# A two-block transformer kernel: rows kept in natural column order through the expert layers

## What is computed

```python
h = jnp.concatenate([meta, x], axis=1)                     # 16 + 256 rows of 1024
for i in range(2):
    h = layer_norm(ALPHA * h + mixed, ln_g[i, 0], ln_b[i, 0])
    # experts: router on h, two experts per token, blocks of gathered rows
    #   hb = silu(xb @ w_gate[e]) * (xb @ w_up[e]);  y += gate * (hb @ w_down[e])
    ffn = hierarchical_moe(h, w_group, b_group, w_expert, b_expert, w_gate, w_up, w_down)
    h = layer_norm(ALPHA * h + ffn, ln_g[i, 1], ln_b[i, 1])
x = h[:, 16:]                                              # then the second block
```

## Time and profile before

| | |
|---|---|
| median of 3 runs | 2130.85 us |
| the three runs | 2118.84, 2130.85, 4760.82 us |
| the profiled execution | 2120.57 us, its span 2118.8 us |
| TensorE busy (matmuls) | 1641.4 us, 77% of the span |
| VectorE busy | 624.1 us, 29% |
| ScalarE busy | 219.3 us, 10% |
| moved by DMA | 546.00 MB, mean 258 GB/s |
| mean granted TensorE clock | 0.869 of full speed |

### The profile page before, as it was taken

One profiled execution on the slowest core, in us unless ns is written; L12 is line 12 of the kernel. 1 busy time (PEld: TensorE's weight loads), 2 busy tenths in 40 slices (PEclk: granted clock), 3 DMA queues, 4 the chain that ended last, 5 costly groups with the idle time before them and its releaser, 6 DMA issues.

```text
span 2118.8 us, 27169 instructions
## 1 busy us (share of the span) xinstructions
PE 1641.4 (77%) x12015; PEld 1066.4 (50%) x12015; DVE 624.1 (29%) x1449; ACT 219.3 (10%) x488; POOL 171.5 (8%) x173
## 2 busy tenths in 40 slices
PE   7897767776766997466556553668999998999998
PEld 5544444444445855243334322336688445668743
DVE  4633122322213763111111115992211012421002
ACT  2301010000001321000000001000011002311000
POOL 2000100000000000000000002991000001000000
PEclk9985988989898997787778776658999999899999
DMA  9352999999999574999999996122434424323420
GB/s 315 119 199 82 336 419 422 419 422 419 421 421 351 210 294 167 419 418 417 419 418 417 419 423 270 40 80 99 173 126 159 144 92 143 118 102 142 154 79 20
DMA packets 105219, 546.00 MB, mean 258 GB/s; under 512 B 7406, under 2 KB 9518, under 8 KB 86924
## 3 DMA queue, kind: packets, MB, share of 16 engines
q1 hardware_dynamic: 102572, 534.39, 63.6%
q0 software_dynamic: 2528, 9.84, 1.3%
HBM read 534.77 MB, written 9.44 MB: 257 GB/s over the span
## 4 chain that ended last, share of the span: by engine, by line
PE 57%; DMA 29%; DVE 8%; issue 3%; SPq 1%; ACT 1%; POOL 0%; DVEq 0%; POOLq 0%; ACTq 0%
DMA ring<-in_moe_w_up 29%; PE ps L664 16%; PE ps L640 16%; PE ps L685 9%; PE ps L1001 3%; PE ps L705 2%; PE ps L697 2%; PE ps L648 2%; DVE work L1911 2%; PE ps L714 1%; DVE work L1910 1%; DVE work L1900 1%; PE ps L1040 1%; DVE work L1901 1%; SPq L423 1%
## 5 line engine op out<-in xcount | busy, mean ns | idle before, releaser
L685 PE MATMUL ps<-ring,work 128*32 128x256 f32 x3968 | 297.2, 466 | 285.1 <-DMA ring<-in_moe_w_up 284.0
L685 PEld LDWEIGHTS ps<-ring,work 128*32 128x32 f32 x3968 | 166.2, 133 | 412.0 <-issue 371.3
L664 PE MATMUL ps<-ring,work 128*128 128x512 f32 (+1 forms) x800 | 346.7, 596 | 13.1 <-DVE work L1830 9.2
L640 PE MATMUL ps<-hT,ring 128*128 128x256 f32 (+2 forms) x1488 | 330.9, 385 | 3.4 <-DMA ring<-in_lru_w_in 3.4
L640 PEld LDWEIGHTS ps<-hT,ring 128*128 128x128 f32 x1488 | 284.4, 192 | 48.5 <-issue 6.7
L664 PEld LDWEIGHTS ps<-ring,work 128*128 128x128 f32 (+1 forms) x800 | 149.0, 187 | 208.0 <-issue 202.4
L1701 DVE TENSOR_TENSOR rowb<-rowb,ps 128x128 f32<-128x128 f32 x64 | 18.4, 288 | 448.3 <-ACT rowb L1226 448.3
L697 PE MATMUL ps<-ring,multi 128*32 128x256 f32 x2016 | 121.8, 382 | 13.5 <-ACT multi L1228 12.8
L705 PE MATMUL ps<-rowb,hres 128*128 128x128 f32 (+1 forms) x640 | 107.9, 311 | 8.0 <-DVE rowb L1453 8.0
L1703 DVE COPY multi<-ps 128x256 f32<-128x256 f32 x64 | 27.2, 424 | 280.3 <-PE ps L697 280.3
L705 PEld LDWEIGHTS ps<-rowb,hres 128*128 128x128 f32 (+1 forms) x640 | 89.2, 204 | 25.1 <-DVE rowb L1453 8.3
(11 more groups left out here) (382 smaller groups left out, 1488.2 us busy)
## 6 DMA issues: line engine op xcount, KB each, us to landing
ring<-in_moe_w_down SPq DMA_DIRECT2D x63, 2048.0 KB, 24.2
ring<-in_moe_w_gate SPq DMA_DIRECT2D x62, 2048.0 KB, 19.4
ring<-in_moe_w_up SPq DMA_DIRECT2D x62, 2048.0 KB, 24.0
ring<-in_w_ff SPq DMA_DIRECT2D x32, 2048.0 KB, 8.4
ring<-in_sc_w_in SPq DMA_DIRECT2D x6, 2048.0 KB, 17.8
ring<-in_lru_w_in SPq DMA_DIRECT2D x4, 2048.0 KB, 18.7
s_rotations<-work POOLq DMA_DIRECT2D x8, 1024.0 KB, 5.1
ring<-s_rotations SPq DMA_DIRECT2D x4, 2048.0 KB, 15.4
```

The costliest lines, as they stand in the source:

```text
L640: mm = pe.matmul(ps[:, bank, 0:n], w[:, k, P * c:P * c + P], hT[:, k, t0:t0 + n], start=(k == 0), stop=(k == DC - 1))
L664: mm = pe.matmul(ps[0:m, 2 + 2 * b + hf, :], left[:, kk, t0:t0 + m], w[:, k, 512 * hf:512 * hf + 512], start=(kk == 0), stop=(kk == 4 * la ...
L685: mm = pe.matmul(ps[32 * q:32 * q + 32, bank, 0:256].rearrange("p (u n) -> p u n", u=2), x[:, k, :], gu[:, k, :, P * q:P * q + P], start=( ...
```

## The change

The rows of an expert layer stay in natural column order. The mix norms write `hres` plainly. The stationary matrices of the mix norms' transposes and of `dispatch` are taken at a stride instead: slab k is `hres[0:m, b, k:D:DC]`, every eighth column. `hT` and the gathered rows hold the same values as before. The residual sum reads `hres` in order, in one instruction per block, with the four PSUM banks as a second dimension. The copy of the meta rows and its wait are gone; TensorE turns them out of `hres` directly.

```diff
-        meta_rows = region(1024, 1024)[0:NMETA]
...
-        def packed(ap):
-            return ap.rearrange("t (p k) -> t k p", k=DC)
-        def unpacked(ap):
-            return ap.rearrange("t (k p) -> t p k", k=DC)
         def two(ap, k):
-            return ap.rearrange("t (a b) -> t a b", b=k)
+            return ap.rearrange("t (a b) -> t a b", a=k)
...
-            def transposes(n, blocks, hold, only=None, bank=0):
+            def transposes(n, blocks, hold, only=None, bank=0, by=1):
...
-                        for c in range(4):
-                            mm = pe.transpose(ps[:, bank + j % 2, c * P:c * P + m], hres[0:m, b, (4 * h + c) * P:(4 * h + c + 1) * P],
+                        for c in range(4 * h, 4 * h + 4):
+                            chunk = slice(c * P, c * P + P) if by == 1 else slice(c, D, by)
+                            mm = pe.transpose(ps[:, bank + j % 2, (c % 4) * P:(c % 4) * P + m], hres[0:m, b, chunk],
                                               ident[0:m, 0:m])
...
-                        mm = pe.matmul(ps[:, bank, width * (k - k0):width * (k - k0) + width], hres[0:m, b, P * k:P * k + P],
+                        mm = pe.matmul(ps[:, bank, width * (k - k0):width * (k - k0) + width], hres[0:m, b, k:D:DC],
                                        one_hot[0:m, i, 0:width], start=(i == 0), stop=(i == len(blocks) - 1), skip_group_check=True)
...
-                    transposes(f"mix{l}", blocks, f"mix{l}_normed", only=i)
+                    transposes(f"mix{l}", blocks, f"mix{l}_normed", only=i, by=DC)
...
-                        pe.wait_ge(*nth("meta_rows", 1))
                         for c in range(DC):
-                            mm = pe.transpose(ps[:, 6, NMETA * c:NMETA * c + NMETA], meta_rows[:, P * c:P * c + P], ident[0:NMETA, 0:NMETA])
+                            mm = pe.transpose(ps[:, 6, NMETA * c:NMETA * c + NMETA], hres[0:NMETA, 0, P * c:P * c + P], ident[0:NMETA, 0:NMETA])
...
-            def to_packed(x, dst, bias):
-                return packed(x), two(dst, P), packed(bias)
...
-                mix_norm(f"mix{l}", to_packed)
+                mix_norm(f"mix{l}")
...
-                    if l == 0 and e == 0:
-                        V.tensor_copy(two(meta_rows, DC), unpacked(hres[0:NMETA, 0, :])).then_inc(S("meta_rows"), 1)
...
-                    for q in range(4):
-                        ins = V.scalar_tensor_tensor(out=x[:, 256 * q:256 * q + 256].rearrange("t (p k) -> t p k", k=DC),
-                                                     in0=unpacked(hres[:, b, :])[:, 32 * q:32 * q + 32, :], scalar=ALPHA,
-                                                     in1=ps[:, q, SEQ * i:SEQ * i + SEQ].rearrange("t (p k) -> t p k", k=DC),
-                                                     op0=ALU.mult, op1=ALU.add)
-                    link(ins)
+                    link(V.scalar_tensor_tensor(out=two(x, 4), in0=two(hres[:, b, :], 4), scalar=ALPHA,
+                                                in1=ps[:, 0:4, SEQ * i:SEQ * i + SEQ], op0=ALU.mult, op1=ALU.add))
```

## The result

| kernel | median us | range | ratio to before, 95% interval |
|---|---|---|---|
| before | 2124.74 (9 runs) | 2118.84 to 2130.85, one of 4760.82 | 1 |
| changed | 2134.61 (9 runs) | 2129.39 to 2139.36 | 1.0047 [1.0029, 1.0064] |

The forecast was a gain of 3 us; the change costs 10. The time lies inside the forecast range and within 2% of before, but the direction was wrong. The execution of 4760.82 us is left out of the ratio. The spans of the two profiled executions are 2129.6 and 2118.8 us. They differ by 10.8, about as the medians do, so the traces can be laid side by side.

The account below looks back on a forecast made before the run. The weight stream bounds the expert loops; single-file work before and after it bounds the rest. VectorE gains of 3.26 us less 0.2 us for strided loads gave -3.1 us from 2120.57, so 2117.5 us, range 2112 to 2139.

Parts of the forecast that it names:

- VectorE's gains: Plain mix norm writes save 1.58 us and one-piece residual sums in layer 1 save 1.68 us, together 3.26 us.
- Layer 0's residual: Residual sum after layer 0's experts: about 0.84 us saved per block, hidden behind TensorE's work, so gain nothing.
- The price of one load: Strided stationary loads on TensorE: 0.91 ns per value, free cold, 5 ns extra for each of 32 warm loads, 0.2 us.
- the bound from two streams: All 1.81 ns per value charged to a strided TensorE load: 232 ns a load, 5.4 us in all.
- rival 1: Small price: TensorE's strided loads pay what VectorE pays for strides, +5.5 us against -3.26, 2122.8 us; chance 27%.
- The slack of the loops: Expert loops: TensorE slack of 107 and 152 us absorbs added dispatch time; only one in-loop dispatch, in layer 1, counts.
- 420 GB/s as before: Weight stream inside the expert loops keeps its rate of 420 GB/s.
- the three signs of being wrong: Cold strided load clearly over 213 ns; stream drying up at other places; layer 0's L910 coming earlier.
- First dispatch of layer 0: Forecast 15.0 us; about 16 to 17.5 under rival 1, about 25 under rival 2.
- Warm loads: Strided loads in layer 1's dispatch at the high clock: period of 111 to 116 ns, against 160 to 232.
- rival 2: Double loads: each of the 112 counted dispatch and transpose loads twice as long, +20.6 us, kernel 2137.9 us; chance 12%.
- The clock: Granted clock steps may be caught earlier or later by shifted stages: a few us either way, 1.6 us in layer 1's dispatch.

Follow-up runs that it names:

- the loads alone: Whole computation left out, TensorE alone running fp32 products and transposes at several column distances; a product's load at distance 8 took 238 ns for 128 columns.
- the best version: Changed kernel with ScalarE copying the two large blocks so their dispatch loads are contiguous, and in-loop dispatch behind down: 2119.04 us, 0.9969 of before.

## Why the prediction was wrong, step by step

- **VectorE's gains: right.** 1285 ns for 2077, and one residual for four. Layer 0's residual was hidden as said: there L901 (L910 before) starts at 666.88 against 666.32. Up to 816 us the change is 0.25 us ahead. The two norm writes gave their 1.58 us and layer 0's first dispatch took 1.2; the rest is a start 0.7 us ahead by scatter (146.65 against 147.36), 0.4 us in layer 0's first gate and up, and 0.5 us lost by the end of its loop.
- **The price of one load: wrong by a factor of two.** This is the first step that failed. The text took 0.91 ns per value, since "a load is one stream", and had 1.81 ns as the bound from two streams. Measured are 1.86. The error was to read the copy L1705, one stream on VectorE, as the nearest row. TensorE's own instructions spoke already: in the kernel before, at the higher clock, a product's load takes 111 ns and a transpose of the meta rows 62, so a product's load is not like one stream. By the forecast's own count the term is then 80 x 27 + 32 x 127 ns = 6.2 us instead of 0.2 (16 of the 80 are transposes, which cost nothing; without them 5.8), and the sum 2123.5 us: rival 1, given 27%.
- **The Trainium skill's rule was the right warning.** First the rows: distance 2 takes 118 ns, 3 173, 4 233, 16 218. With fp32, two neighbouring values at a distance of 2 share 16 bytes, and from a distance of 4 none do. At a distance of 3 one pair in four values shares them, and 173 ns is halfway between 112 and 233. The Trainium skill's Advanced Engine Details and Errata, section SBUF Cachelines, states such a rule: lines of 16 bytes, two hits needed on each to hide the memory's latency, and a penalty where every access falls on another line. The trace agrees for products on where the step lies; the page gives no price. For transposes the trace has no such step (120 ns at distances 2 and 4, 110 at 8), so it is not shown that the rule is the mechanism. The forecast cited it and gave it weight only in the rivals.
- **The slack of the loops: the second step that failed**, and the larger one. The forecast put the dispatches inside the loops at nothing: it divided a whole loop's slack (107 us in layer 0) by its loads and counted a single dispatch of layer 1. The runs put 9 to 10 us on them. But slack is not the same everywhere: the issue of the next down load waits for down, down stands behind the dispatch in TensorE's queue, and in layer 1 the gate and up loads queue behind that down load on SP. So 2.0 us are added to one chain in each group of four experts, and the stream was barely kept full there (375 GB/s at 911 to 914 us in the kernel before). The forecast saw this place once, at 848 us, and did not ask whether it returns. It does, six times more. The run with the dispatch behind down shows it: 11 us back at the same work, against 4 in the kernel before.
- **"420 GB/s as before"**: right for layer 0 (421), wrong for layer 1 (409). Two of the three signs of being wrong came: a cold period clearly over 213 ns (240), and a stream that dries up at other places.
- **First dispatch of layer 0**: 16.17 us, in rival 1's 16 to 17.5. **Warm loads**: 237 ns, just beyond its 160 to 232, and so the doubling of rival 2; cold loads grew by 27 ns alone, and rival 2's 25 us for this dispatch didn't come.
- **The clock**: named as "a few us either way", and so it was: 1.7 us in layer 1's first gate and up, seen with contiguous loads too.
- **The range held by luck.** It reached to 2139 us for rival 2 and for scatter; neither the price nor the waits in the loops were what filled it. Also, the forecast started from one fast execution (2120.57 us), 4 us below the median before.

## What to carry to other kernels

In these runs a product's stationary matrix of 128 columns that lie 4 or more fp32 values apart cost 1.7 to 1.9 ns per column whatever the clock. Compare that with the matmul that runs over it: at clock 1.00 it shows with fewer than some 280 moving columns, an estimate (128 x 1.86 / 0.84 ns, from 429 ns for 512). Put the layout change where an idle engine can do it, not on the one that sets the end.

A queue's slack must be counted for each chain, not for a stage: take the instruction that releases the next transfer and list what stands ahead of it in its engine's order. Work that nobody waits for, as the next group's gather here, goes behind that instruction; it was worth 4 us even in the kernel before.

## What the runs showed of the hardware that I had not expected

- The time of a product's load at distance 8 hardly depends on the granted clock: 240 ns at 0.50, 237 at 1.00, in the kernel and in the loads alone.
- Every second fp32 value costs nearly nothing (118 against 112 ns), every third 173 ns, every fourth the full 233, every sixteenth a little less (218).
- ScalarE pays as well. Instruction groups of the best version, 790 to 830 us:

```profile
L1207 ACT ACTIVATE hT<-hres 128x1024 f32<-128x1024 f32 x2 | 3.9, 2020 | 0.0
...
L1218 ACT ACTIVATE work<-ps 128x1024 f32<-128x1024 f32 x1 | 1.0, 1024 | 2.3 <-PE ps L788 2.3
```

  1024 columns take 2020 ns when read with a distance of 8, and 1024 ns when contiguous. (The contiguous ones come from the accumulators, `ps`, so a part of the difference could be the source.) The strided read is 1.97 ns per value, close to TensorE's price and to VectorE's two streams (1.81). VectorE's single strided stream, L1705, had taken 1237 ns.
- The clock's steps at layer 1's first products come at different moments from execution to execution, and move 3 us: dispatch, then gate and up, took 5.50 + 3.63 us in one and 6.64 + 5.14 us in another, both with contiguous loads. In the first the clock rose to 1.00 and stayed; in the second it rose 2.4 us later and fell back to 0.50 in gate and up.
